# Attention scores as one four-byte matmul per head and block of queries, in place of three single-pass matmuls of rounded parts

## The reference, cut to what matters

```python
q = rmsnorm_2(q.reshape(b, s, ATTN_HEADS, HEAD_DIM), q_norm_w)
k = rmsnorm_2(k.reshape(b, s, ATTN_HEADS, HEAD_DIM), k_norm_w)
...
logits = jnp.einsum('bhnqd,bhnkd->bhnqk', qr, kblk,
                    preferred_element_type=jnp.float32) * (dh ** -0.5)
logits = jnp.where(mask[None, None], logits + bias[None, :, None], NEG)
p = jnp.exp(logits - m)
o = jnp.einsum('bhnqk,bhnkd->bhnqd', p, vblk) / denom
```

## Time and profile before

| | |
|---|---|
| time, median of 3 runs | 1527.88 us (1527.62 to 1528.46) |
| the profiled execution's own time | 1527.15 us |
| its span, first to last instruction | 1525.4 us |
| TensorE, share of the span busy | 99% |
| VectorE | 53% |
| ScalarE | 48% |
| GpSimd | 44% |
| granted TensorE clock, mean | 1.000 |

### The profile page before, as it was taken

How to read it: one execution, slowest core, us unless ns; L and a number is a source line. 1 busy time by engine, 2 the same in 40 slices (tenths; PEclk the granted TensorE clock), 3 DMA queues, 4 the chain that set the end, 5 groups by cost and what they waited for, 6 DMA issues and landing times.

```text
span 1525.4 us, 20918 instructions
## 1 busy us (share of the span) xinstructions
PE 1512.7 (99%) x7180; PEld 1237.5 (81%) x7180; DVE 809.7 (53%) x1388; ACT 731.8 (48%) x1172; POOL 665.1 (44%) x509
## 2 busy tenths in 40 slices
PE   7999999999999999999999999999999999999999
PEld 6888888888888888888878888888888887777777
DVE  5677778442346741577633445555542335756761
ACT  6667665323346532466654344444443344545551
POOL 5334333444544454343344444444455544434432
PEclk9999999999999999999999999999999999999999
DMA  6222222232222233222223332333333343222212
GB/s 245 84 70 81 71 70 71 95 97 84 97 79 74 69 97 96 83 70 83 70 84 97 97 97 96 96 96 96 96 97 107 102 136 104 82 95 94 82 57 96
DMA packets 39399, 140.87 MB, mean 92 GB/s; under 512 B 4312, under 2 KB 4824, under 8 KB 39328
## 3 DMA queue, kind: packets, MB, share of 16 engines
q1 hardware_dynamic: 37664, 134.89, 27.7%
q10 hardware_dynamic: 1664, 5.01, 0.9%
HBM read 137.76 MB, written 2.13 MB: 92 GB/s over the span
## 4 chain that ended last, share of the span: by engine, by line
PE 98%; DMA 1%; DVE 0%; issue 0%; SPq 0%; ACT 0%; DVEq 0%
PE bank L504 27%; PE bank L508 27%; PE bank L507 27%; PE bank L732 3%; PE bank L1020 3%; PE bank L605 1%; PE bank L759 1%; PE bank L939 1%; PE bank L929 1%; PE bank L920 1%; DMA oneh<-onehot 1%; PE bank L658 0%; PE bank L1011 0%; PE bank L515 0%; PE bank L573 0%; PE bank L660 0%
## 5 line engine op out<-in xcount | busy, mean ns | idle before, releaser
L445 POOL TENSOR_TENSOR wl<-raw,wh 128x512 fp32r<-128x512 f32 x490 | 646.4, 1341 | 842.8 <-ACT wh L1063 830.6
L504 PE MATMUL bank<-hh,wh 128*128 128x512 f32 x840 | 333.9, 398 | 0.0
L508 PE MATMUL bank<-hh,wl 128*128 128x512 f32 x840 | 327.8, 390 | 0.0
L507 PE MATMUL bank<-hl,wh 128*128 128x512 f32 x840 | 327.2, 390 | 0.0
L504 PE MATMUL bank<-yh,wh 128*128 128x512 f32 x800 | 314.6, 393 | 0.0
L1063 ACT ACTIVATE wh<-raw 128x1024 fp32r<-128x1024 f32 x241 | 252.9, 1051 | 124.2 <-DMA raw<-slabs 124.0
L508 PE MATMUL bank<-yh,wl 128*128 128x512 f32 x800 | 311.5, 389 | 0.0
L507 PE MATMUL bank<-yl,wh 128*128 128x512 f32 x800 | 311.5, 389 | 0.0
L508 PEld LDWEIGHTS bank<-hh,wl 128*128 128x128 f32 x840 | 157.6, 188 | 33.9
L504 PEld LDWEIGHTS bank<-hh,wh 128*128 128x128 f32 x840 | 157.9, 188 | 33.0 <-issue 1.4
L507 PEld LDWEIGHTS bank<-hl,wh 128*128 128x128 f32 x840 | 158.0, 188 | 31.4
(11 more groups left out here) (356 smaller groups left out, 2022.7 us busy)
## 6 DMA issues: line engine op xcount, KB each, us to landing
raw<-slabs SPq DMA_DIRECT2D x245, 512.0 KB, 3.5
xs<-x SPq DMA_DIRECT2D x4, 512.0 KB, 5.7
xT<-xt SPq DMA_DIRECT2D x4, 512.0 KB, 12.8
wb<-bias_scratch ACTq DMA_DIRECT2D x1, 1792.0 KB, 8.7
wb<-bias_scratch ACTq DMA_DIRECT2D x2, 896.0 KB, 4.3
out<-a_l SPq DMA_DIRECT2D x4, 256.0 KB, 4.7
out<-au SPq DMA_DIRECT2D x3, 256.0 KB, 2.0
con<-consts ACTq DMA_DIRECT2D x1, 767.0 KB, 7.0
```

The source lines that it names most:

```text
L445: pool.tensor_tensor(slab(wl, i, half), slab(raw, i, half), slab(wh, i, half).bitcast(F32), ALU.subtract).then_inc(S["slab_split"], 1)
L504: mm(bank[:, :], wh[:, s, b, :], xh, start=first and i == 0, stop=False)
L507: mm(bank[:, :], wh[:, s, b, :], xl, start=False, stop=False)
L508: ins = mm(bank[:, :], wl[:, s, b, :], xh, start=False, stop=last and i == len(order) - 1)
```

## The change

`at_scores` makes one matmul for each head, with plain float32 operands: the stationary one is `a_q` (the turned queries, now kept in four bytes), the moving one the normalised keys in `au[t % 2][r, 1, :]` themselves. `at_round` keeps only the copy that turns the queries; the rounding of the keys and both subtractions are gone, with `at_rest`, the semaphore `at_nl` and the tiles `a_ql`, `a_kh`, `a_kl`. The wait ahead of part 0 is for the normalised keys (`at_n`) and the turned copy (`at_nh`).

```diff
-        a_qh = sec("a_qh", [P, T], F32R)
+        a_q = sec("a_q", [P, T])
...
-        a_kh = sec("a_kh", [P, T], F32R)
         late = stage(rsn_at)
-        a_ql = late("a_ql", [P, T], F32R)
-        a_kl = late("a_kl", [P, T], F32R)
...
             def at_scores(q, t):
                 wait(pe, S["at_l"], 8 * t + 2 * q)
-                for k, (a, b) in enumerate(((a_qh, a_kh), (a_qh, a_kl), (a_ql, a_kh))):
-                    for hd in range(2):
-                        r = head_rows(hd)
-                        ins = mm((b5, b6)[hd][:, :], a[r, q * P:(q + 1) * P], b[r, :], start=k == 0, stop=k == 2)
-                        if k == 2:
-                            ins.then_inc(S["at_s"], 1)
+                for hd in range(2):
+                    r = head_rows(hd)
+                    mm((b5, b6)[hd][:, :], a_q[r, q * P:(q + 1) * P], au[t % 2][r, 1, :], start=True, stop=True
+                       ).then_inc(S["at_s"], 1)
...
                 if part == 0:
-                    pe.wait_ge(S["at_nl"], 2 * t + 2)
+                    pe.wait_ge(S["at_n"], 2 * t + 2)
+                    pe.wait_ge(S["at_nh"], t + 1)
                     pe.wait_ge(S["at_rs"], 4 * t + 4)
...
             def at_round(t):
-                q, k = au[t % 2][:, 0, :], au[t % 2][:, 1, :]
                 wait(dve, S["at_s"], 8 * t)
                 dve.wait_ge(S["at_n"], 2 * t + 2)
-                dve.tensor_copy(turned(a_qh[:, :]), q.rearrange("p (b t) -> p b t", b=NB)).then_inc(S["at_nh"], 1)
-                dve.tensor_copy(a_kh[:, :], k).then_inc(S["at_nh"], 1)
-
-            def at_rest(t):
-
-                q, k = au[t % 2][:, 0, :], au[t % 2][:, 1, :]
-                dve.wait_ge(S["at_nh"], 2 * t + 1)
-                TT(a_ql[:, :].rearrange("p (b t) -> p b t", b=NB), turned(q),
-                   a_qh[:, :].bitcast(F32).rearrange("p (b t) -> p b t", b=NB), ALU.subtract).then_inc(S["at_nl"], 1)
-                dve.wait_ge(S["at_nh"], 2 * t + 2)
-                TT(a_kl[:, :], k, a_kh[:, :].bitcast(F32), ALU.subtract).then_inc(S["at_nl"], 1)
+                dve.tensor_copy(turned(a_q[:, :]), au[t % 2][:, 0, :].rearrange("p (b t) -> p b t", b=NB)
+                                ).then_inc(S["at_nh"], 1)
```

More of the change, by code:

```diff
@@ L205, in build @@
             cv_z cv_c cv_y cv_hi cv_lo
-            at_silu at_sq at_sl kbr_set at_ss at_tr at_rs at_v at_n at_nh at_nl at_s at_l at_mx at_ex at_sum at_p at_pt at_o at_y
+            at_silu at_sq at_sl kbr_set at_ss at_tr at_rs at_v at_n at_nh at_s at_l at_mx at_ex at_sum at_p at_pt at_o at_y
             at_hi at_lo out_sum out_ev out_dma""".split()
@@ L2445, in _ @@
                     at_round(0)
-                    at_rest(0)
                 if t < 3 and part >= 2:
@@ L2463, in _ @@
                     at_normalise(i, t)
-                if t < 3 and part == 3:
-                    at_rest(t + 1)
                 if part == 1 and t:
```

## The result

The changed kernel takes 1530.47 us (median of 22 runs, 1529.93 to 1531.64), the kernel before 1527.99 us (22 runs, 1527.32 to 1528.62). The ratio is 1.0017 with a 95% interval of 1.0011 to 1.0023: 2.5 us slower, clear of no change, but less than the 0.2% that were taken as the limit of a difference. The profiled execution took 1530.46 us, with a span of 1528.7.

A forecast was written before the change was run, and what follows sets the result against it. TensorE's steps from start to start were taken to bound the kernel. Score blocks +2.72, less 0.17 of waiting, gave +2.55 on 1527.88: 1530.4 us; likeliest case 1528.9 to 1532.1, whole range 1527.4 to 1537.5.

The forecast's parts named there:

- Two rounds shared by the heads: In each of 16 score blocks both heads' four-byte matmuls share two rounds: 1.06 us against 0.89; chance 0.78.
- The neighbours it was priced from: Trace steps bounding the new score block: full-width four-byte matmuls, values, line 535's lookups (0.96 us) and the present scores.
- open load: At a score block's start, loading 128 columns of weights uncovered costs 0.10 to 0.11 us; 64 columns cost 0.05.
- way out: At a score block's end, the array empties before it goes back to full width: 0.09 us.
- The load of the second round: In the new score block, taken as hidden under the first round; a block is 1.17 us if it stood open.
- The serial case: Rival: in the scores the heads run one after the other, four rounds, 1.92 us a block, 1543.5 us; chance 0.11.
- The staggered case: Rival: the second head's scores start with the first's second round, three rounds, 1.49 us a block, 1536.9 us; chance 0.08.
- One round for a four-byte instruction: Rival: a half-row four-byte score matmul needs one round, 0.63 us a block, 1523.7 us; chance 0.03.
- VectorE's work: The removed rounding of the keys and both subtractions (subtractions 9.8 us) delayed no matmul: gain 0.
- The 0.4 us wait by a weight load: Ahead of the first score block, the stretch's only wait on the removed work; it delayed no matmul.
- The wait at 1470 us: TensorE waits for VectorE at the transposes; reaching them 0.17 us later, it waits 0.17 less; ends 0 and -0.9.
- The two waits: At the transposes, a step of 0.63 for 0.23 and four taking 0.97 for some 0.45: together 0.9 us.

The follow-up runs named there:

- half of the keys: The changed kernel with scores for the first 256 of the 512 keys alone: 1524.29 us in one run.
- head-by-head order: The kernel before with the score loops swapped, all three single-pass products of the first head, then all three of the second: 1528.29 us in one run.

## Why the prediction was right

**The sum.** 1530.4 us forecast, 1530.47 measured. Two rounds shared by the heads, 1.06 us a block: measured 1.0595. The block before: 0.89 read, 0.8944 over all. The difference was put at 0.17 and is 0.165, which makes 2.64 in place of 2.72. The sum has no term for the 0.19 us in the matmuls between the blocks, so by the traces the change costs 2.65 us and not 2.55. The mechanism and its main term were right; that the forecast came within 0.1 us is luck, since the runs of one kernel range over more than 1 us.

**The neighbours it was priced from.** The first round (0.53) is 0.43 and an open load of 0.107 us, the last (0.53) is 0.43 and a way out of 0.10 (0.09 in the prediction), as added up from the values with 64 columns of weights, the old scores with 128, and the lookups with 64 rows. The load of the second round was taken as hidden, and half of the keys showed it hidden even under a round half as long.

**The rivals.** The serial case was refuted by the trace of the changed kernel and its price confirmed by putting both heads on one half. The staggered case was refuted too, and the head-by-head order points to the reason, which the prediction did not have: it argued from the values alone that pairs share their rounds. Had the records been started in strict order, instruction by instruction, the new scores would have been staggered. One round for a four-byte instruction is out, with 64 records for 32.

**VectorE's work.** Priced at nothing, and keeping it made no difference. The 0.4 us wait by a weight load was rightly not counted.

**The wait at 1470 us.** The 0.17 us that it gives back are the difference of 0.63 and 0.45 in the two steps. That the wait belongs to VectorE's chain behind the projection, not to the scores, is shown by moving the convolution's product away. The two waits were put at 0.9 us together; with the whole convolution moved, 0.97 us came back.

**What was off.** The durations of the new matmul records were to be near 0.59 us; their median is 0.64. These are modelled ends and nothing hung on them. The waits at the transposes were to shrink from 0.6 to 0.4 and show as 0.3. "Matmuls elsewhere follow each other without a wait" overlooked 0.3 us at 1255 us and 0.2 us at 13.3 us, which changes nothing in the sum. VectorE's busy time was to fall by the subtractions and casts and nothing else to change. They are 11.5 us of 14.2. Most of the rest is one product of the convolution, which the edit doesn't touch, first before and then after:

```profile
L2427 DVE TENSOR_TENSOR c<-c,c 128x512 f32<-128x512 f32 x4 | 6.0, 1498 | 0.0
```

```profile
L2413 DVE TENSOR_TENSOR c<-c,c 128x512 f32<-128x512 f32 x4 | 2.7, 685 | 0.0
```

With the old VectorE work kept it takes 1498 ns again. Why was not tried, and no matmul waited for it in the two kernels of the change.

## What to carry to other kernels

Where TensorE is the bound, a native four-byte matmul is worth taking for its simplicity only if the rounds allow it: on this chip it is two rounds at half pace, 0.43 us each for 512 columns, against 0.23 for each single-pass product, so it beats four products and loses to three. Pair matmuls on different halves of the array before anything else; that was worth 0.85 us a block here, five times what the change adds to one. Before counting on work taken off another engine, look for a matmul that waits for it; and when one wait is removed, look at what the moved work delays next.

## What the runs showed of the hardware that was not expected

- Matmuls on different halves of the rows are started independently of their order in the program: three and three in a row gave three shared rounds, 0.90 us, not five of 1.34.
- The opening varies from run to run, with the clock. The 24 transposes at the start, 128 columns each, come at 0.21 us at first and at 0.11 later. The page gives a granted clock of 1.00 throughout, but the trace's own record of the granted clock begins only at 11.66 us in the trace of before and at 13.24 us in that after, and that is where the steps halve. In all eleven traces the record begins between 11.66 and 14.34 us, within 0.2 us of the change of pace; in the two latest (14.14 and 14.34 us) all the transposes are at 0.21 us. Half the pace fits the lower level of the clock, 1.2 GHz, though no record gives the clock of that first stretch. The opening after, in order of time, against the lookups' start at 13.34 us before:

```profile
9.03 4.88 PE L526 MATMUL bank<-con,xn 128*128 128x128 f32 x24 [9.03 <-DVE xn L1678]
13.84 1.03 PE L532 MATMUL bank<-oneh,par 64*8 64x512 f32 x4
14.80 0.50 PE L501 MATMUL bank<-hh,wh 128*128 128x512 f32 x1
```

Over eleven profiled executions of eleven kernels TensorE's transposes begin between 8.91 and 9.22 us, and the lookups that follow them (line 535 before) between 13.34 and 14.33 us. That is a spread of 1 us, which is 40% of this change, beside ranges of 0.95 to 2.25 us among the 10 to 22 runs of one kernel. What makes the clock rise earlier or later was not tried. When two profiled executions are compared, their offset ahead of the change has to be read and taken off first: here it was 0.7 of 3.3 us.
